# Modulation vectors made in three parts of 2048 columns on four column tiles, in three stages

## The reference

```python
mod_x = (jax.nn.silu(c) @ ada_w + ada_b)[:, None, :]
mod_c = (jax.nn.silu(c_ctx) @ ada_w + ada_b)[None, None, :]
sh1x, sc1x, g1x, sh2x, sc2x, g2x = jnp.split(mod_x, N_MOD, axis=-1)
sh1c, sc1c, g1c, sh2c, sc2c, g2c = jnp.split(mod_c, N_MOD, axis=-1)
zx = modulate(rmsnorm(x, norm1_g), sh1x, sc1x) @ w_in
zc = modulate(rmsnorm(ctx, norm1_g), sh1c, sc1c) @ w_in
```

## Time and profile before

| | |
|---|---|
| runs of the kernel before | 4402.25, 4390.68, 4398.53 us; median 4398.53 |
| profiled execution | 4391.63 us, of which the span of the profile is 4390.0 us |
| PE busy | 3438.7 us (78%) |
| DVE, ACT, POOL busy | 2098.2, 1188.0, 184.2 us |
| mean DMA rate | 128 GB/s |

### The profile page before, as it was taken

How to read it: one execution, slowest core, us unless ns; L and a number is a source line. 1 busy time by engine, 2 the same in 40 slices (tenths; PEclk the granted TensorE clock), 3 DMA queues, 4 the chain that set the end, 5 groups by cost and what they waited for, 6 DMA issues and landing times. The chain is left out here.

```text
span 4390.0 us, 52510 instructions
## 1 busy us (share of the span) xinstructions
PE 3438.7 (78%) x18825; PEld 2720.3 (62%) x18826; DVE 2098.2 (48%) x2999; ACT 1188.0 (27%) x1808; POOL 184.2 (4%) x262
## 2 busy tenths in 40 slices
PE   7599882077585898988847987974947998998977
PEld 1388772066364777766625876962835887787855
DVE  0411014834523756577743113836643775576543
ACT  0401002123422645566622002333122110011021
POOL 1000000013101000000010000000000000000000
PEclk9799995578796999999968998996978999999988
DMA  7232210349454967699922322111020332232211
GB/s 249 71 93 85 84 58 12 102 155 244 162 188 181 326 235 277 238 333 333 336 92 67 96 86 72 40 39 51 4 72 25 95 94 83 86 91 86 86 52 44
DMA packets 394400, 562.01 MB, mean 128 GB/s; under 512 B 43373, under 2 KB 277540, under 8 KB 394148
## 3 DMA queue, kind: packets, MB, share of 16 engines
q1 hardware_dynamic: 350392, 431.46, 30.6%
q10 hardware_dynamic: 26784, 69.74, 4.4%
q0 software_dynamic: 17104, 59.17, 3.6%
HBM read 451.51 MB, written 108.79 MB: 128 GB/s over the span
## 5 line engine op out<-in xcount | busy, mean ns | idle before, releaser
L1760 DVE TENSOR_TENSOR exp_w_lo<-exp_w_raw,exp_w_hi 128x1024 fp32r<-128x1024 f32 x384 | 450.4, 1221 | 145.9 <-ACT exp_w_hi L1734 143.4
L1734 ACT ACTIVATE exp_w_hi<-exp_w_raw 128x1024 fp32r<-128x1024 f32 x384 | 382.1, 1051 | 176.5 <-DMA exp_w_raw<-in_expert_w_in 155.9
L325 PE MATMUL in_ps_psum<-hN_hi,in_wh 128*128 128x512 f32 x704 | 276.1, 392 | 40.0 <-DVE in_wl L319 40.0
L325 PE MATMUL up_ps_psum<-hN_hi,up_wh 128*128 128x512 f32 x704 | 281.6, 400 | 31.2 <-DVE up_wl L319 31.2
L326 PE MATMUL up_ps_psum<-hN_lo,up_wh 128*128 128x512 f32 x704 | 281.1, 399 | 0.0
L327 PE MATMUL up_ps_psum<-hN_hi,up_wl 128*128 128x512 f32 x704 | 280.9, 399 | 0.0
L326 PE MATMUL in_ps_psum<-hN_lo,in_wh 128*128 128x512 f32 x704 | 275.7, 392 | 0.0
L327 PE MATMUL in_ps_psum<-hN_hi,in_wl 128*128 128x512 f32 x704 | 275.2, 391 | 0.0
L325 PE MATMUL exp_up_psum<-exp_w_hi,exp_x_hi 128*128 128x512 f32 x592 | 235.9, 399 | 11.1 <-DVE exp_w_lo L1760 10.4
L317 DVE CAST in_wh<-in_w 128x1024 fp32r<-128x1024 f32 x44 | 30.5, 694 | 425.6 <-PE in_ps_psum L327 414.2
L326 PE MATMUL exp_up_psum<-exp_w_lo,exp_x_hi 128*128 128x512 f32 x592 | 231.4, 391 | 0.0
(11 more groups left out here) (604 smaller groups left out, 7534.9 us busy)
## 6 DMA issues: line engine op xcount, KB each, us to landing
exp_w_raw<-in_expert_w_in SPq DMA_DIRECT2D x256, 512.0 KB, 5.4
exp_w_raw<-in_expert_w_out SPq DMA_DIRECT2D x128, 512.0 KB, 6.1
up_w<-in_ffn_up SPq DMA_DIRECT2D x88, 512.0 KB
moe_rows<-zero_rows ACTq DMA_DIRECT2D x50, 512.0 KB, 2.7
ada_w<-in_ada_w SPq DMA_DIRECT2D x12, 2048.0 KB, 8.0
in_w<-in_w_in SPq DMA_DIRECT2D x44, 512.0 KB, 4.2
down_w<-in_ffn_down SPq DMA_DIRECT2D x44, 512.0 KB
exp_rows<-moe_rows POOLq DMA_DIRECT2D x39, 512.0 KB, 7.7
```

What stands on the lines that cost most here:

```text
L325: pe.matmul(out, r(w[0]), r(x[0]), start=start, stop=False)
L1734: act.activation(wh[:, c, :].bitcast(F32R), raw[r][:], ACT.Copy).then_inc(s_wh, 1)
L1760: dve.tensor_tensor(wl[:, c, :].bitcast(F32R), raw[r][:], wh[:, c, :], ALU.subtract).then_inc(s_wl[r], 1)
```

## The change: one function for 2048 columns, called in three stages

`ada_part(K, st, g)` makes columns 2048g to 2048g+2047. It returns one piece of code for SP, one for PE and one for DVE. SP loads eight tiles of 128 rows x 2048 columns (1 MB each) into four buffers, tile k waiting for the products of tile k-4, and then the bias, one DMA for each 512 columns and row. PE multiplies tile k by `cond_silu[:, k, 0:R]`, four products of 512 columns, each written to its own 32 partitions of one PSUM bank (partitions 0, 32, 64, 96). R is 2 in part 0 (x and ctx) and 1 in the others. DVE adds the bias in four instructions; PE turns the sums with 16 small products against corners of the identity; DVE copies them to `modcols`. The way through DRAM and the products for ctx that nobody reads are gone. Part 0 is in `stage_setup` in the place of the twelve slices, ahead of the turn of the weight vectors; part 1 in the norm of x, on PE and DVE behind the norm's own work; part 2 in `stage_misc`, on SP between the four loads and the store, on PE behind the 120 products, on DVE behind the two copies. `cond_silu` is kept for the whole program.

```diff
--- before.py
+++ after.py
+def ada_part(K, st, g):
+    A, name, NR, NW, R = K.A, f"ada{g}", 4, 512, 2 if g == 0 else 1
+    w = [K.sb(f"{name}_w{i}", [P, 4, NW], stack=st) for i in range(NR)]
+    bias, out = K.sb(f"{name}_bias", [P, NW], stack=st), K.sb(f"{name}_out", [P, NW], stack=st)
+    pm, pt = K.ps(f"{name}_sum", [P, NW], st), K.ps(f"{name}_turn", [P, 4, BANK], st)
+    s_w = [K.sem(f"{name}_w{i}") for i in range(NR)]
+    s_bias, s_mm, s_all, s_ev, s_t, s_col = (K.sem(f"{name}_{x}") for x in ("bias", "mm", "sums", "biased", "turned", "cols"))
+    at = lambda j: slice(32 * j, 32 * j + R)
+    def sync(sp):
+        for k in range(KT):
+            if k >= NR:
+                sp.wait_ge(s_mm, k - NR + 1)
+            sp.dma_start(w[k % NR][:], A["ada_w"][0, k * P:(k + 1) * P, g * 2048:(g + 1) * 2048].rearrange("p (j n) -> p j n", j=4)) \
+                .then_inc(s_w[k % NR], 16)
+        for j in range(4):
+            for r in range(R):
+                c = g * 2048 + j * NW
+                sp.dma_start(bias[32 * j + r:32 * j + r + 1, :], A["ada_b"][:, c:c + NW]).then_inc(s_bias, 16)
+    def tensor(pe):
+        for k in range(KT):
+            pe.wait_ge(s_w[k % NR], 16 * (k // NR + 1))
+            for j in range(4):
+                mm = pe.matmul(pm[at(j), :], K.csil[:, k, 0:R], w[k % NR][:, j, :], start=k == 0, stop=k == KT - 1)
+            mm.then_inc(s_mm, 1)
+        pe.wait_ge(s_ev, 4)
+        for j in range(4):
+            for i in range(4):
+                mm = pe.matmul(pt[:, j, i * R:(i + 1) * R], out[at(j), i * P:(i + 1) * P], K.c("ident")[at(j), at(j)], start=True, stop=True)
+        mm.then_inc(s_t, 1)
+    def vector(dve):
+        dve.wait_ge(s_bias, 16 * 4 * R)
+        dve.wait_ge(s_mm, KT)
+        for j in range(4):
+            dve.tensor_tensor(out[at(j), :], pm[at(j), :], bias[at(j), :], ALU.add).then_inc(s_ev, 1)
+        dve.wait_ge(s_t, 1)
+        for r in range(R):
+            c = 48 if r else 16 * g
+            t = pt[:, :, 0:4 * R].rearrange("p j (i r) -> p j i r", r=R)[:, :, :, r]
+            dve.tensor_copy(K.modcols[:, c:c + 16].rearrange("p (j i) -> p j i", j=4), t).then_inc(s_col, 1)
+        dve.wait_ge(s_col, R)
+        for o in ((8, 56), (), (32,))[g]:
+            dve.tensor_scalar(K.modcols[:, o:o + 8], K.modcols[:, o:o + 8], 1.0, None, ALU.add)
+    return sync, tensor, vector
...
@@ stage_setup
+    K.csil = K.sb("cond_silu", [P, 8, 2])
...
-                sp.dma_start(K.const[:], K.const_dram).then_inc(s_const, 16)
                 sp.dma_start(crow[0:8, :], flat_rows(A["c"], P)).then_inc(s_cond, 16)
                 sp.dma_start(crow[8:16, :], flat_rows(A["c_ctx"], P)).then_inc(s_cond, 16)
-                for r in range(2):
-                    sp.dma_start(brow[r:r + 1, :], A["ada_b"]).then_inc(s_bias, 16)
-                for n in range(12):
-                    if n >= NW:
-                        sp.wait_ge(s_mm, n - NW + 1)
-                    sp.dma_start(aw[n % NW][:], A["ada_w"][0, :, n * 512:(n + 1) * 512].rearrange("(k p) n -> p k n", p=P)) \
-                        .then_inc(s_aw[n % NW], 16)
-                sp.wait_ge(s_ev, 12)
-                sp.dma_start(mod, mout[:]).then_inc(s_mod, 16)
-                sp.wait_ge(s_mod, 16)
-                sp.dma_start(mrows[0:48, :], flat_rows(mod[0:1, :], P)).then_inc(s_modrows, 16)
-                sp.dma_start(mrows[48:64, :], flat_rows(mod[1:2, 0:2 * D], P)).then_inc(s_modrows, 16)
+                sp.dma_start(K.const[:], K.const_dram).then_inc(s_const, 16)
+                ada_sync(sp)
...
-                for n in range(12):
-                    pe.wait_ge(s_aw[n % NW], 16 * (n // NW + 1))
-                    if n >= 2:
-                        pe.wait_ge(s_ev, n - 1)
-                    for k in range(8):
-                        mm = pe.matmul(pm[n % 2][:], csil[:, k, :], aw[n % NW][:, k, :], start=k == 0, stop=k == 7)
-                    mm.then_inc(s_mm, 1)
+                ada_tensor(pe)
                 pe.wait_ge(s_rows, 16 * len(pieces))
                 for i in range(ntile):
                     mm = pe.transpose(pt[:, i * P:(i + 1) * P], rows[i][:], K.c("ident"))
                 mm.then_inc(s_t, 1)
-                pe.wait_ge(s_tc, 1)
-                pe.wait_ge(s_modrows, 32)
-                pe.transpose(pt[:, 0:64], mrows[:], K.c("ident")[0:64, 0:64]).then_inc(s_t, 1)
...
-                dve.wait_ge(s_bias, 32)
-                for n in range(12):
-                    dve.wait_ge(s_mm, n + 1)
-                    dve.tensor_tensor(mout[:, n * 512:(n + 1) * 512], pm[n % 2][:], brow[:, n * 512:(n + 1) * 512],
-                                      ALU.add).then_inc(s_ev, 1)
+                ada_vector(dve)
                 dve.wait_ge(s_t, 2)
                 dve.tensor_copy(K.cols[:], pt[:]).then_inc(s_tc, 1)
-                dve.wait_ge(s_t, 3)
-                dve.tensor_copy(K.modcols[:], pt[:, 0:64]).then_inc(s_tc, 1)
-
-                dve.wait_ge(s_tc, 2)
-                for o in (8, 32, 56):
-                    dve.tensor_scalar(K.modcols[:, o:o + 8], K.modcols[:, o:o + 8], 1.0, None, ALU.add)
...
@@ stage_norm
+def stage_norm(K, name, src, dst, ntok, gain, shift=None, scale=None, ada=None):
...
+        if ada is not None:
+            ada_sync, ada_tensor, ada_vector = ada_part(K, st, ada)
...
+                if ada is not None:
+                    ada_tensor(pe)
+
+            if ada is not None:
+                @block.sync
+                def _(sp):
+                    ada_sync(sp)
...
+                if ada is not None:
+                    ada_vector(dve)
...
@@ stage_misc
+        ada_sync, ada_tensor, ada_vector = ada_part(K, st, 2)
...
                     sp.dma_start(wm[:, :, o:o + n], w[:, :, c:c + n]).then_inc(s_w, 16)
+                ada_sync(sp)
                 sp.wait_ge(s_cp, 2)
...
                 mm.then_inc(s_mm, 1)
+                ada_tensor(pe)
 
...
                 dve.tensor_copy(ob[:, 0:NCTX], flat[:, T:TALL]).then_inc(s_cp, 1)
+                ada_vector(dve)
...
@@ mixer_one
-            stage_norm(K, "n1x", K.hF, K.x, T, g1, shift=mc[:, 0:8], scale=mc[:, 8:16])
+            stage_norm(K, "n1x", K.hF, K.x, T, g1, shift=mc[:, 0:8], scale=mc[:, 8:16], ada=1)
```

More of the change, by code:

```diff
@@ L177, in stage_setup @@
         at += n
-    mod = K.dram("mod", [2, 6 * D])
     with K.stage() as st:
         rows = [K.sb(f"vec_rows{i}", [P, P], stack=st) for i in range(ntile)]
-        mrows = K.sb("mod_rows", [64, P], stack=st)
         crow = K.sb("cond_rows", [16, P], stack=st)
[L183 to L187, removed]
-        pt = K.ps("vec_ps", [P, ntile * P], st)
[L189 to L193, removed]
+        ada_sync, ada_tensor, ada_vector = ada_part(K, st, 0)
+        pt = K.ps("vec_ps", [P, ntile * P], st)
+        s_const, s_rows, s_cond, s_t, s_tc, s_zero, s_sil = (
+            K.sem(f"setup_{x}") for x in ("const", "rows", "cond", "turned", "copied", "zero", "silu"))
         pieces = []
@@ L232, in _ @@
                 act.wait_ge(s_t, 1)
-                act.activation(csil[:].rearrange("p k r -> p r k"), pt[:, 0:16].rearrange("p (r k) -> p r k", r=2),
+                act.activation(K.csil[:].rearrange("p k r -> p r k"), pt[:, 0:16].rearrange("p (r k) -> p r k", r=2),
                                ACT.Silu).then_inc(s_sil, 1)
@@ L327, in matmul3 @@
     return pe.matmul(out, r(w[1]), r(x[0]), start=False, stop=stop)
-def stage_norm(K, name, src, dst, ntok, gain, shift=None, scale=None):
+def stage_norm(K, name, src, dst, ntok, gain, shift=None, scale=None, ada=None):
     W = min(512, ntok)
```

## The result

The changed kernel takes 4348.65 us (median of 4 runs, 4344.81 to 4356.4), the kernel before 4395.2 us (4 runs, 4390.68 to 4402.25): a ratio of 0.9893, 95% interval 0.9877 to 0.991. That is 46.6 us less. The forecast was 43 us less, 4355 with a range of 4340 to 4371. The profiled execution is the longest of the four, 4356.4 us with a span of 4354.9.

The account below looks back on a forecast made before the run. Setup was taken as bound by PE, the norm of x by ACT and DVE, the small projection by a chain; -68.3 + 6.8 + 18.5 = -43.0 us from 4391.6, plus 6.9 for the median, gave 4355, range 4340 to 4371.

Parts of the forecast that it names:

- Setup: Setup stage: its last instruction would end at 39.6 us instead of 107.94, with transfers and a bare tail; -68.3 us.
- the turn: Turning a part's sums on PE: sixteen turns of two records at 0.112 us each, 3.6 us.
- Norm of x: Norm of x: the eight tiles are hidden, only DVE's and PE's exchange behind the norm is added; +6.8 us.
- Small projection: Small projection: tiles 4 to 7 come only after the 120 products, and a tail follows; +18.5 us.
- Four side by side: New products in all three parts: four column tiles overlap, records 0.109 us apart, so a part needs 7.0 us of PE.
- Two at a time: New products: only two column tiles overlap, spacing 0.218 us, about +3 us on the forecast, 4358 us; chance 0.27.
- The narrow loads suffer: Small projection: weight tiles share engines with the `misc_w` loads, split starts up to 10.9 us later; 4366 us; chance 0.13.
- No overlap: New products: column tiles don't overlap, a part takes 27.5 us of PE, total gain 12.6 us, 4386 us; chance 0.08.
- Each waits for the end: New products: each record waits for its predecessor's whole 0.60 us, a part takes 38.4 us; 4418 us, slower; chance 0.04.
- The clock: PE's clock in the parts: products awaiting transfers run cold, by the skill's rule about 1 us less gain than forecast.

Follow-up runs that it names:

- The second profile: The changed kernel run again with no edit: 4352.7 us, ratio 0.9905 to the kernel before.
- the run with the short tail and the convolution: Changed kernel with one addition and four full turns per part, and part 2 moved from small projection to convolution stage: 4322.05 us, ratio 0.9827.
- the experiment that makes it so: Changed kernel with a tile's four products on two column tiles and two PSUM banks instead of four column tiles: 4356.0 us, ratio 0.991.

## Why the prediction was right

*Setup, -68.3 forecast, -66.7 measured.* The last tile's products began at 30.30 where 30.0 had been set for its landing. The products took 1.89 (1.8), the additions 2.84 (2.7), the turns 4.50 (3.6), copies, scales and hand-overs 1.6 (1.5), and the gap to the next stage was 0.8, as before. The term that was off is the turn: 0.141 us a record instead of 0.112 taken from small turns in one pass each; one weight load lasts 0.33 us here and 0.22 for the turns of the earlier trace rows. Why they last longer no run tried. One step of the forecast was wrong without a price here: tile 7 and the bias were asked for near 22 us, not 19, since PE ended tile 3 at 22.1, and in the profiles whose last tile ran at full clock the bias is seen to land after it, not before or with it. Here the products of the last tile, at half clock, covered that.

*Norm of x, +6.8 forecast, +6.8 measured.* The agreement to a tenth is luck. The order was as forecast: tiles 0 to 3 without a wait, tiles 4 to 7 just ahead of DVE. Bias and copies came 0.1 or 0.2 us from their prices, but the turns cost 0.9 more, and what stands behind DVE's last subtraction grew by 7.8 us (8.54 against 0.72), not 6.8. In this profile the norm's own work up to there was 1.0 us shorter than in the first one of before (40.93 against 41.97 from the stage's start), and that hid the miss. The second profile has 41.90 and a stage of 50.45, and two experiments with the same norm have 50.92 and 50.39: about +8 us over the 42.5 of before. The hiding has less room than the first profile shows, too: the last products ended 1.5 us ahead of DVE's last subtraction there, 0.4 in the second, and in the run with the short tail and the convolution 0.15 us behind it, where DVE waited 0.28.

*Small projection, +18.5 forecast, +20.0 measured.* Products ended at 621.95, 16.2 us behind the 120 (16.1 forecast); the turns cost 0.9 more, the narrow loads 0.8 more than before. Seven buffers showed that the wait stood for buffers, as the prediction had it.

*Four side by side.* The step on which all rested, taken from two rows on other tiles, was right to 1%: 0.108 against 0.109. One column tile shows its price at the total, +35.5 us, where +30 had been expected; by the stages, what is above it lies in the slower turns and in products at half clock.

*The rivals.* "Two at a time" is refuted by the fours, though the experiment that makes it so ends within the noise of the changed kernel. "The narrow loads suffer" is refuted at its price of up to 10.9 us: with `ada_w` asked for behind the narrow loads the split comes 4.7 to 5.6 us after the first of them (six profiles, mean 5.1), without 4.6 to 4.9 (six, mean 4.7). Some 0.4 us may be real. "No overlap" is what one column tile builds, at 4384 where 4386 had been forecast for it. "Each waits for the end" is refuted by the changed kernel itself, where the tile changes with every product and records are 0.108 apart, not 0.60.

*The clock.* The row on the last tile shows 0.55 where PE had waited between bursts. The Trainium skill ("TensorE: Matmul & The Clock Gate", Loop structure matters more than you think) warns that products behind a long wait for a DMA run cold. The trace agrees in part: the tile ahead of the last one in setup took 1.04 us, at the full clock, behind a wait of 0.72, and in the small projection the first awaited tile took 1.04 behind a wait of 2.39, the next three 1.88 or 1.89 at 0.50. So the forecast, which took 1.8 for every last tile, was a fair price and not a rule. Half clock cost 1.89 instead of 1.04 us on an exposed tile, and 4.50 (clock 0.50) instead of 3.13 (0.76 on the mean) on the turns.

*The total.* -40.0 for the three stages, where -43.0 was forecast, with medians 46.6 us apart, and 42.6 in the second comparison (4352.7 against 4395.28). The intervals of the two ratios overlap over most of their length, and what lies behind the stages scatters by more. So the stages give 3 us less than forecast, the turns being the largest miss (0.9 us in each part). That the total came out beyond the forecast instead is not explained by the stages, and lies within the scatter.

## What to carry to other kernels

Products with few stationary columns can lie side by side on column tiles, and then the transfers set the time; check next whether the weights can be loaded beside a stage that leaves both SP and PE idle, with enough buffers that no tile waits for PE. What is left bare is the tail, so write it with few instructions over all partitions, and put it where its engine would wait anyway. Of a part moved into a stage, count only what ends behind that stage's own chain: here 64 records and 8 MB cost nothing in the norm, with at most 2 us to spare, and nine microseconds for want of buffers in the small projection.

## What the hardware showed that was not expected

- Granted clock can take back what tiling gives: two fours at 1.2 GHz take the 1.89 us for a tile that four pairs take at 2.4 GHz. On four tiles the last burst of setup was granted either clock (1.89 down to 1.04 us in seven profiles).
- The records of one fp32 product don't run one behind the other on column tiles: four records run at once, by inference the first passes of all four products, then the second ones.
- Early in a trace the column PEclk shows 1.00 while records stand at half clock: at 12.02 eight records of the changed kernel take 1.89 us, as at 30.30 with 0.55, and at 25.30 still 1.77. There the durations are to be read and not the column.
- Sixteen turns of a 2 x 128 block take 6.98 us from one group of rows and 4.50 from four groups, both at a clock of 0.50; from four groups 3.13 at a mean of 0.76 (one row each, R = 1). Four turns of 128 x 128 take 0.66 at 1.00 and 1.12 at 0.50.
